# Copying the first layer's queries to the other 64 partitions by DMA from SBUF to SBUF instead of by GpSimd

## What is computed

```python
# first layer ("even"): one input projection, two head groups
qa, ka, va, ga, qs, ks, vs, gs = split_cols(x @ w_in, EVEN_SPLITS)
# A: differential attention with ALiBi, 4 heads x 2 maps, d = 64
s = einsum(qb, ka) * 64**-0.5 - slope * |tq - pos|
p = softmax(where(visible, s, -inf));  w = p[map 0] - lam * p[map 1]
ya = rms_norm(w @ va, subln_g) * (1 - lam_init) * silu(ga)
# B: stick-breaking attention, 8 heads, d = 64
z = einsum(qb, ks) * 64**-0.5
a = where(earlier, exp(log_sigmoid(z) + log_pass), 0)
ys = (a @ vs) * silu(gs)
h = layer_norm(ALPHA * h + concat([ya, ys]) @ w_out)
```

## Time and profile before

| | |
|---|---|
| median of three runs | 1342.43 us (1340.15 to 1342.68) |
| the profiled execution, its own time | 1342.14 us |
| its span, from first to last instruction | 1340.2 us |
| outside the span | 1.9 us |
| mean granted PE clock | 0.996 |
| PE busy | 1294.9 us, 97% of the span |
| DVE / ACT / POOL busy | 871.3 / 565.2 / 477.1 us |

### The profile page before, as it was taken

The page is one execution under the profiler, slowest core; times in us unless marked ns, Lnnn a source line. Parts: engine busy times, 40 slices in busy tenths (PEclk is TensorE's granted clock), DMA queues, the critical chain, the costliest instruction groups (busy, mean ns, idle before and its releaser), DMA issues.

```text
span 1340.2 us, 22174 instructions
## 1 busy us (share of the span) xinstructions
PE 1294.9 (97%) x8228; PEld 1221.5 (91%) x8228; DVE 871.3 (65%) x1959; ACT 565.2 (42%) x1332; POOL 477.1 (36%) x461
## 2 busy tenths in 40 slices
PE   8999999999999999998999999998999999999997
PEld 7999998999899999997888999998999989998886
DVE  5685868586677848669555323654778677776455
ACT  3444646364744535356101012533565545656200
POOL 3323221233224142246533324563333234334531
PEclk9999999999999999998999999999999999999999
DMA  6001010101010111214233311122111112115242
GB/s 227 33 28 36 17 49 32 49 33 48 33 40 25 37 45 52 63 29 137 68 126 126 111 32 61 66 83 75 36 48 45 48 44 64 41 46 194 69 161 79
DMA packets 46922, 88.25 MB, mean 66 GB/s; under 512 B 4048, under 2 KB 29648, under 8 KB 46688
## 3 DMA queue, kind: packets, MB, share of 16 engines
q1 hardware_dynamic: 44368, 78.45, 17.8%
q10 hardware_dynamic: 2448, 8.39, 1.6%
HBM read 66.84 MB, written 19.98 MB: 65 GB/s over the span
## 4 chain that ended last, share of the span: by engine, by line
PE 82%; DVE 9%; ACT 5%; issue 2%; POOL 1%; DMA 1%; DVEq 0%; SPq 0%; ACTq 0%; POOLq 0%
PE bank L2023 41%; PE bank L2174 13%; PE bank L2091 11%; PE bank L2146 8%; PE bank L2113 6%; DVE ring L1808 2%; DVE pb L1790 1%; PE bank L2062 1%; PE bank L2131 1%; ACT rtmp L1390 1%; DVE big L1607 1%; PE bank L2196 1%; DVE big L1847 1%; DVE tb L1737 1%; ACT vtok L1426 1%
## 5 line engine op out<-in xcount | busy, mean ns | idle before, releaser
L2023 PE MATMUL bank<-big,wsp 128*128 128x344 f32 (+2 forms) x3024 | 550.4, 327 | 8.4 <-DVE big L1607 4.5
L2023 PEld LDWEIGHTS bank<-big,wsp 128*128 128x128 f32 x3024 | 481.1, 189 | 15.0 <-POOL wsp L1067 4.2
L1066 POOL TENSOR_SCALAR wsp<-wraw 128x1024 fp32r<-128x1024 f32 (+4 forms) x92 | 84.3, 917 | 529.7 <-PE bank L2023 414.9
L1808 DVE TENSOR_TENSOR ring<-bank,ring 128x512 fp32r<-128x512 f32 (+3 forms) x280 | 154.9, 569 | 71.6 <-ACT ring L1477 44.8
L2174 PE MATMUL bank<-big,wsp 128*128 128x512 f32 x800 | 191.5, 397 | 1.5 <-DVE big L1847 1.2
L2174 PEld LDWEIGHTS bank<-big,wsp 128*128 128x128 f32 x800 | 149.3, 188 | 36.4 <-DVE big L1847 1.7
L1067 POOL TENSOR_TENSOR wsp<-wraw,wsp 128x1024 fp32r<-128x1024 f32 (+4 forms) x92 | 179.3, 1949 | 7.7
L2023 PE MATMUL bank<-h1t,wsp 128*128 128x344 f32 (+2 forms) x1080 | 173.9, 322 | 1.4 <-DVE lraw L1655 1.4
L2023 PEld LDWEIGHTS bank<-h1t,wsp 128*128 128x128 f32 x1080 | 170.2, 188 | 3.6 <-DVE lraw L1655 1.7
L1477 ACT ACTIVATE ring<-bank 128x512 fp32r<-128x512 f32 (+1 forms) x200 | 106.0, 555 | 112.8 <-PE bank L2113 80.4
L2146 PE MATMUL bank<-ring,vtok 128*128 128x256 f32 (+1 forms) x1040 | 143.3, 279 | 2.0 <-DVE ring L1808 1.0
(11 more groups left out here) (138 smaller groups left out, 1497.6 us busy)
## 6 DMA issues: line engine op xcount, KB each, us to landing
wraw<-in_w SPq DMA_DIRECT2D x47, 512.0 KB, 3.4
wraw<-y_scratch SPq DMA_DIRECT2D x17, 448.0 KB, 3.8
woraw<-in_wo SPq DMA_DIRECT2D x12, 512.0 KB, 5.3
y_scratch<-ot SPq DMA_DIRECT2D x37, 128.0 KB, 1.7
xres<-in_x SPq DMA_DIRECT2D x8, 512.0 KB, 4.7
h_scratch<-res ACTq DMA_DIRECT2D x8, 512.0 KB, 2.6
gate_scratch<-gtmp SPq DMA_DIRECT2D x8, 512.0 KB, 2.9
gate<-gate_scratch SPq DMA_DIRECT2D x8, 512.0 KB, 3.7
```

What stands on the lines that cost most here:

```text
L1066: pool.wait_ge(S["pool_step"], tick(nc.gpsimd.tensor_scalar(hi, raw, 1.0, 1.0, ALU.mult, ALU.mult)))
L1808: V.tensor_tensor(to, bank[T_BANK[t]][from_, 0:w], lo_hi(R[from_, r % NRING, 0, 0:w]), ALU.subtract)\
L2023: ins = mm(dst, wsp[:, SLOT[kind, u], a, k, :], rhs[:, b, k0 + k, c0:c0 + w], start=(k == 0 and a == 0 and b == 0), stop=last)
```

## The change

The 48 POOL instructions that copy the first layer's queries are gone. In their place SP waits for the evacuation of a chunk and issues two DMAs from `qst` rows 0 to 63 to `qst` rows 64 to 127, one for each map or head: 64 rows by two parts by 352 (or 344) columns of 4 bytes, 176 KB (172 KB) each. Each chunk has a semaphore of its own, and PE waits until both DMAs of this unit have landed. The second layer's copies (`qr`) stay on POOL. The planner now assumes 130 ns on SP and a tail of 2300 ns for such a copy, and so gives a new order for the first layer's attention.

```diff
-RANK = {..., "pool": "CDGQVWO", "sp": "FLO"}
+RANK = {..., "pool": "CDGQVWO", "sp": "QFLO"}
...
-            after += [("pool", copied)] if copied in within else []
+            after += [("pool" if layer else "sp", copied)] if copied in within else []
...
-            L.put("pool", "Q", s, 1790 if kind == "q0" else 1000, [("dve", s)], 20)
+            if kind == "q0":
+                L.put("sp", "Q", s, 130, [("dve", s)], 2300)
+            else:
+                L.put("pool", "Q", s, 1000, [("dve", s)], 20)
...
+                    if s[1] == "q0":                      # in SP's loop over its list
+                        c0, w = CHUNKS[s[3]]
+                        sp.wait_ge(S["proj_evac"], EVAC_AT[s])
+                        for m in range(2):
+                            sp.dma_start(lo_hi(qst[64:128, m, :, c0:c0 + w]), lo_hi(qst[0:64, m, :, c0:c0 + w]))\
+                                .then_inc(S[f"q_moved_{s[3]}"], 16)
...
-                    pe.wait_ge(S["q_copied"], Q_COPY["P", "qr" if layer else "q0", u - u % 2 if layer else u, cq])
+                    if layer:
+                        pe.wait_ge(S["q_copied"], Q_COPY["P", "qr", u - u % 2, cq])
+                    else:
+                        pe.wait_ge(S[f"q_moved_{cq}"], 32 * (u + 1))
```

More of the change, by code:

```diff
@@ L260 @@
 NEAR = {"pe": 0, "act": 0, "dve": 0, "pool": 0, "sp": 0}
-RANK = {"pe": "SXTVp", "act": "TSEYQPW", "dve": "PTSMCYFWO", "pool": "CDGQVWO", "sp": "FLO"}
+RANK = {"pe": "SXTVp", "act": "TSEYQPW", "dve": "PTSMCYFWO", "pool": "CDGQVWO", "sp": "QFLO"}
 class Lines:
@@ L651, in count_before @@
     return out
-Q_COPY = count_before(PROJ, lambda s: s[1] in ("q0", "qr"))
+Q_COPY = {s: n * (32 if s[1] == "q0" else 1) for s, n in
+          [*count_before([s for s in PROJ if s[1] == "q0"], lambda s: True).items(),
+           *count_before([s for s in PROJ if s[1] == "qr"], lambda s: True).items()]}
 ROTATED = count_before(PROJ, lambda s: s[1] in ("kpe", "qr"))
@@ L855, in trunk_kernel @@
             w_raw_0 w_raw_1 w_ready y_split wo_hi wo_split_pool wo_split_dve
-            wo_in_0 wo_in_1 wo_in_2 wo_in_3 wo_in_4 wo_in_5 wo_in_6 wo_in_7 proj_done proj_hi proj_evac proj_read rotated rms_log rms_inverse q_copied lat_sq lat_add lat_sum lat_root lat_norm lat_split
+            wo_in_0 wo_in_1 wo_in_2 wo_in_3 wo_in_4 wo_in_5 wo_in_6 wo_in_7 proj_done proj_hi proj_evac proj_read rotated rms_log rms_inverse q_moved_0 q_moved_1 q_moved_2 q_copied lat_sq lat_add lat_sum lat_root lat_norm lat_split
             s_done s_free_dve s_free_act max_ready exp_done inverted v_cleared v_stepped y_gated p_ready_dve p_ready_pool
@@ L1167, in copy_queries @@
                 for m in range(2):
-                    if kind == "q0":
-                        to, from_ = qst[64:128, m, :, cc], qst[0:64, m, :, cc]
-                    elif m == 0:
+                    if m == 0:
                         to, from_ = qpe[64:128, m, 0, cc], qpe[0:64, m, 0, cc]
@@ L1236, in _ @@
                         clear_meta_values(1)
-                if s[0] == "P" and s[1] in ("q0", "qr"):
+                if s[0] == "P" and s[1] == "qr":
                     copy_queries(s)
```

## The result

The changed kernel takes 1357.46 us (median of 4, 1355.75 to 1358.68), the kernel before 1342.56 beside it: ratio 1.0117, interval 1.0104 to 1.013. It is 15 us slower; 1339.6 was predicted, in a range of 1335.5 to 1346.0. The profiled execution took 1358.18 us, with a span of 1356.3.

What follows compares the result with a forecast made beforehand. PE's work was taken to bound the kernel (1294.9 of 1340.2 us busy). From 1342.14 us, -3.0 (copy waits) -0.3 (DVE) +0.6 (unit 0) +0.2 (unit 4) = -2.5 gave 1339.6 us, range 1335.5 to 1346.0.

Steps and rivals of the forecast that it cites:

- What is removed, -3.0: PE's waits on POOL's query copies, 37 to 612 us: 3.0 us won, taken between 2.45 and 3.3.
- the two named waits: PE's waits for late POOL copies in unit 6 chunk 2 (1.59 us) and unit 5 chunk 1 (0.86 us).
- 0.3 us of relief for DVE: DVE no longer held up by POOL's 48 copies; a tenth of its time counts, 0.3 us won.
- L = 2.3 us, at most 3.1: Latency from DVE's end to the second DMA's landing, taken as 2.3 us, bounds 2.05 to 3.1.
- my sum by the issue: Second estimate of the copies' latency: 1.81 for one, plus 0.33 for an issue, plus 0.03 for SP: 2.17 us.
- Half rate: Rival, chance 0.22: 64-row copies land late, latency 3.1 us, costing 6.8 against 3.3 won: +3.5, 1345.6 us.
- Margins of 0.2 to 0.5 us at eleven places: Units 1 to 7, first scores close behind copies: margins left sum to 4.4 us, so none waits at 2.3 us latency.
- Unit 0 was priced at 0.6 us: Unit 0, chunk 0: same order, PE has nothing else, so its first score starts 0.6 us later.
- The new order itself, 2 us either way: Rival, chance 0.11: up to 612 us PE's changed list makes softmax chains start later; priced 2 us either way.
- SP as a queue at nothing: Loads and stores behind SP's waits cost nothing; unit 2 chunk 2's copy about 2 us late, with some 10 us spare.
- the signs of the half rate: Profile after: median landing above 2.5 us, and PE's waits for the query DMA above 4 us in sum.
- After 612 us within 1 us: Sign: after 612 us the traces before and after the change agree within 1 us.

Runs made afterwards that it cites:

- e6: Kernel before, its order kept, with only the four query chunks that POOL made late sent by DMA, cut by part: 1339.01 us against 1341.02, ratio 0.9985.
- e8: Separate kernel that copies x to out and times single transfers of different shapes; the second of a pair lands 3.4 us after the first one's issue.
- e4: Changed kernel, but the planner assumes 1240 ns on SP and a tail of 2150 ns for a copy pair: 1357.38 us, ratio 1.012.
- e2: Kernel before with POOL still making the copies, but with the changed kernel's new order: 1351.42 us, ratio 1.0081.
- e7: Kernel before with one planner number changed, a POOL query copy taken as 2000 ns instead of 1790: 1357.24 us, ratio 1.0123.
- e9: Kernel before, copies on POOL, with the new order in units 1 to 3 alone: 1344.28 us, ratio 1.0024.
- e15: e9 with POOL's low-part split of unit 2's gate weights made for one of eight blocks: 1341.98 us, ratio 1.0003.
- e11: Kernel before, copies on POOL, with the new order only in the tail of the first layer: 1344.55 us, ratio 1.0026.
- e1: Changed kernel's DMA copies, but PE, ACT and DVE in the order of the kernel before: 1353.53 us against 1340.91, ratio 1.009.
- e5: Order of the kernel before, DMA copies cut by part: high parts leave after ScalarE, low parts after VectorE: 1347.02 us, ratio 1.0036.
- e9 to e11: e9, e11 and a run between them: kernel before, copies on POOL, new order in units 5 to 7 alone, 1344.69 us, ratio 1.0021.

## Why the prediction was wrong

- **What is removed, -3.0: right.** e6 shows the two named waits (2.45 us) come back as 2.3 in the trace and 2.0 in the median. The 0.3 us of relief for DVE were not seen anywhere.
- **L = 2.3 us, at most 3.1: the mis-sized term.** It is 3.47 in the trace, above even the high end. I took issue, fixed part and rate from stores of 128 rows. In e8's numbers, from the 2.17 of my sum by the issue: +0.31 for a second issue after 0.64 us and not 0.33, +0.7 for 64 rows in two pieces (2.5 against 1.8 us), +0.25 for the second of two back to back: 3.4. "Half rate" was a rival with the right mechanism; its end was too low because issue and first packet depend on shape as well.
- **Margins of 0.2 to 0.5 us at eleven places: right, and they fix the price.** With L 1.15 longer, 11 x 1.15 - 4.4 = 8.3, plus 1.75 for unit 0 and 1.35 for unit 4: 11.4 us of waits by the prediction's own rule. PE waited 9.9: 0.53 to 0.85 us at eight places of units 1 to 7, 1.91 in unit 0, and 1.73 in unit 2, where a fetch of instructions made the copy 1.2 us later.
- **Waits cost their own length: right only while the clock stays up.** No term was there for the clock. Unit 0 was priced at 0.6 us. It had a wait of 1.91 us and then 6.83 us at 0.50, and cost 4.6; the same wait with no low clock behind it cost 1.8 (e4). What decides which of the two comes is not known from these runs.
- **"The new order itself, 2 us either way", chance 0.11: the second error, and as large.** e2 has it at +10.5 us and e7 a mere number at +16. I had priced it by the longest single waits. But the list that stood there was one of many and a good one; in another list PE waits at other places. Two are taken apart: 2.3 us where POOL's split met DVE's combining instruction (e9, e15), and about 3.3 us where four matmuls stand ahead of the last products (e11).
- **SP as a queue at nothing: right.** No weight load came late: in after POOL never waited for `wraw` between 18 and 650 us. The copy that was to be about 2 us late behind a load (unit 2, chunk 2) was issued 0.03 us after DVE's end, like the 23 others. A load some 1 us behind a copy's second issue cost it little: landing after 2.9 us in units 1 and 3, and 3.3 in unit 4, where a fetch of 8 KB ran too.
- **The signs.** Landing after 2.8 us (above 2.5) and 9.9 us of waits (above 4) were the signs of the half rate, and the copies were late; but that rival alone stood at 1345.6. POOL's busy time fell by 40 us, where 43 was expected.
- **"After 612 us within 1 us": wrong.** From unit 7's queries to the last products 3.9 us were lost, of which 2.1 came back; the tail is part of the planned stretch (e11).

The two causes are shown apart (e1, e2) and in their parts (e5, e8; e9 to e11, e15). Of their overlap, 12.6 + 10.5 alone and 15 together, 6.7 us are waits on copies; the rest, and when the low clock comes, is not settled.

## What to carry to other kernels

Price a transfer by its own shape (rows, pieces a row, how many behind one another), not by a neighbour with 128 rows: together they decided 1.2 us here, twenty-four times. Where an order is written out by a planner, a change of an assumed number is a change of its own and has to be measured by itself, on the old engines, before the new engine is judged; here the useful part of the idea (four copies, old order) wins 2 us and the whole of it loses 15. Where the bounding engine is full, leave room in the range for the clock behind a standstill: here the same wait of 1.9 us cost from 1.8 to 4.6 us.

## What the hardware showed that was not expected

- A fetch of instructions can delay a transfer: copies of 172 to 176 KB with a packet of 16 KB of the instruction queue (0.92 to 1.55 us) in their flight landed after 3.5 to 4.6 us, the others after 2.8 to 3.3.
- The issue itself lasts 0.32, 0.47 or 0.60 us by the shape of the transfer, not by its bytes (8 KB and 176 KB alike at 0.60).
- The same wait of 1.9 us was followed by 6.83 us at a granted clock of 0.50 in one kernel's trace, by 3.41 us in another's and by none in a third's; a wait of 2.7 us by 3.41 us in six traces of eight.
- A DVE instruction with two SBUF operands took 3.1 times as long beside a POOL instruction (2.81 and 0.90 us), while POOL's own took 2.53 us beside it, for 2.39 in the earlier trace rows.
